# Expert blocks of 32 rows on four column tiles of TensorE, and two early weight loads held for the first gather

## The chip, the cores and the metric

The kernel runs on one core of one Trainium2 chip. The metric is device microseconds of one execution, the median of several runs. TensorE multiplies, VectorE and ScalarE do elementwise work and empty PSUM, GpSimd (POOL in the profile) does the gathers, SyncE (SP) issues most DMAs.

## The reference

Two transformer-like blocks over 512 tokens of width 1024, in float32: FFN, two attentions, FFN, then a convolution and mLSTM mixer, and at the end a mixture of experts. The change lies in the last part. 32 experts, each token goes to two of them:

```python
h = xt @ router weights          # group of 8 experts by argmax, then top 2 in the group
for each expert e, its rows xb:
    a, u = xb @ w_gate[e], xb @ w_up[e]          # 1024 x 512 each
    y = (silu(a) * u) @ w_down[e]                # 512 x 1024
out[token] = x[token] + sum over its 2 experts of gate * y
out = rmsnorm(out)
```

The reference's router sends these inputs to the experts in very uneven parts. In the order in which the kernel takes the experts, they get 6, 21, 0, 109, 2, 150, 1, 61, 6, 82, 3, 61, 6, 90, 3, 55, 4, 6, 1, 46, 2, 22, 8, 34, 7, 8, 0, 129, 5, 59, 2, 35 rows, 1024 in all.

## The kernel before

Everything up to the router is not touched, and is not told here. The experts' rows are cut into blocks of `BS` = 64 rows (`MAX_BLOCKS` at most), a block belongs to one expert. Three sets of buffers (`SETS`, chosen by block number modulo 3) each hold one expert's gate, up and down weights of 2 MB each. The blocks run in laps of three, one for each set. The first three experts open the three sets; the others are laid out down the first set's column, then down the second's, then down the third's, so that all blocks of one expert follow each other in the same set, three apart. A set's weights are loaded again only when the expert of its column changes (`need`); an expert that has several blocks keeps its set for as many laps. With 64 rows there are 37 blocks in 13 laps (39 places, two of them empty).

One block `c` on each engine:

- TensorE: `gate_up(c)` (L1737: 8 contraction chunks, each one matmul for gate and one for up, on two column tiles of 64), `next_rows` (L1658: the gathered rows of block c+1 turned), `down(c-1)` (L1752: 4 chunks by two output halves, again on two column tiles), `turn_products(c)` (L1760: gate and up products of block c turned, 4 transposes).
- ScalarE: copies the products out of PSUM (L1766), copies the result of block c-1 (L1777) and issues its two stores to `y_rows` (L1780), and applies silu (L1771).
- VectorE: scales the turned rows (L1699), hands the next row numbers to GpSimd (L1663), multiplies silu and up (L1792).
- GpSimd: gathers the rows of block c+4 once block c+1's have been turned (L1651).
- SyncE: `load_first(c)` issues gate and up of block c after `gate_up(c-3)`, `load_down(c-1)` issues down of block c-1 after `down(c-4)`. All weight loads stand in this one queue, in that order: gate c, up c, down c-1.

Ahead of the loop SyncE loads the first experts. `load_expert(2, 1, 1)` and `load_expert(2, 2, 2)` are the last of these. The router's counts and places are worked out on VectorE, then `gather(0)` is issued, and block 0 can begin. After the loop GpSimd gathers each token's two results from `y_rows`, VectorE adds them, and the output is stored.

Of the kernel before, what the change touches and what calls it, by code (L numbers as in the profile page):

```python
# [32 lines left out]
BS = 64  # L33
MAX_BLOCKS = N_EXP + 2 * T // BS
SETS = 3
NO_ROW = 8 * T
SLOT_COLS = MAX_BLOCKS + 4
# [89 lines left out]
def build(nc, x_d, cols_d, rows_d, wdense_d, wff_d, wif_d, wr_d, strips_d, experts_d, out_d):  # L127
# [15 lines left out]
    s_y = sem("block_results_stored")  # L143
# [72 lines left out]
    iota_f, tok_id = sb("iota_f", 128), sm(2 * NT)  # L216
# [130 lines left out]
    y_d = nc.dram_tensor("y_rows", (MAX_BLOCKS * BS, D), F32).ap()  # L347
# [38 lines left out]
    def ffn(first_in, first_out, ready, gain):  # L386
# [523 lines left out]
    assert RING * SLOT - WE >= 1024 + 8 * BS and 5 * WE <= BIG - 8 * T  # L910
# [578 lines left out]
    sp.wait_ge(PE.sem, PE.n)  # L1489
    load_expert(2, 1, 1)  # L1490
    sp.wait_ge(s_hrow, NT * 16)
# [12 lines left out]
    quota, steps3, multiples = sm(32), sm(MAX_BLOCKS // SETS), sm(8)  # L1504
# [3 lines left out]
    DV.step(dv.tensor_scalar(multiples, iota_f[:, 1:9], float(BS), None, ALU.mult))  # L1508
# [64 lines left out]
    DV.run(dv.tensor_scalar(nb.bitcast(I32), nb.bitcast(I32), 6, None, ALU.logical_shift_right))  # L1573
# [26 lines left out]
    over = work[:, 256:256 + C2 * 8].rearrange("p (c n) -> p c n", c=C2)  # L1600
    DV.run(dv.tensor_tensor(over, over_last(rank, C2, 8), multiples.unsqueeze(1).to_broadcast([128, C2, 8]), ALU.is_ge))
# [12 lines left out]
    oh_tok, oh_exp = work[:, 1952:1952 + C2 * SLOT_COLS], hi_raw[:, 2 * D:2 * D + C2 * SLOT_COLS]  # L1614
    assert C2 * SLOT_COLS <= 416 and 2 * D + C2 * SLOT_COLS <= 2 * SLOT

# [27 lines left out]
    y_e, gu = ring[:, 0:512], ring[:, 512:1024]  # L1644
    hg, het = ring[:, 1024:1024 + 4 * BS], ring[:, 1280:1280 + 4 * BS]
# [60 lines left out]
    take_rows(0, slice(3, 4)).then_inc(DV.sem, 2)  # L1706
    DV.n += 3

    ac.wait_ge(s_fill, 16)
    ac.sem_inc(s_y, 16)  # L1710

    per = {"pe": 4, "ac": 3, "dv": 3}
# [4 lines left out]
    DV_X, DV_IDX, DV_MUL = range(1, 4)  # L1717
# [5 lines left out]
    turned_h = banks[4].rearrange("p (c m s) -> p c m s", c=4, m=2)  # L1723
# [3 lines left out]
    def gate_up(i, c, rows_next=True):  # L1727
# [17 lines left out]
    def down(i, c, steps=1):  # L1745
# [91 lines left out]
    ac.wait_ge(s_y, laps["ac"] * (32 * SETS) + (32 * (SETS - 1) + 16))
    ac.activation(y_e, results[SETS - 1][:, :], ACT.Copy).then_inc(AC.sem, 1)
    ac.wait_ge(AC.sem, at_step(AC, AC_SILU, laps["ac"], 2) + 1)
    for half in range(2):  # L1840
        ac.dma_start(y_d[bass.ds(laps["ac"] * (SETS * BS) + (SETS - 1) * BS, BS), half * 512:half * 512 + 512],
                     y_e[half * BS:(half + 1) * BS, :]).then_inc(s_y, 16)
# [30 lines left out]
    po.wait_ge(s_y, laps["po"] * (32 * SETS) + (32 * SETS + 16))  # L1873
# [151 lines left out]
```

## Time and profile before

| | us |
|---|---|
| median of 3 runs (lowest, highest) | 2067.76 (2067.05, 2069.86) |
| the profiled execution's own time | 2066.26 |
| its span | 2065.0 |
| TensorE busy in the span | 1878.1 |
| bytes read from HBM | 383.84 MB |

The span is what the profile covers; the execution's own time is 1.3 us longer. Start times in the trace are counted from the span's start. An engine's busy time tells how long it had an instruction under way, not that it was at its limit.

### The profile page before, as it was taken

To read this page: it belongs to the slowest core of one execution; us is meant where nothing else is said; L and a number is where in the kernel's file an instruction comes from. 1 tells how busy PE (TensorE), PEld (TensorE's weight loads), DVE (VectorE), ACT (ScalarE), POOL (GpSimd) and SP (SyncE) were. 2 spreads that over 40 slices of the span, in tenths; PEclk is the share of its full clock that TensorE was granted. 3 is DMA by queue.
4 is the path that set the end of the run, shared out by engine and by line. 5 is a ranking of instruction groups with operands and counts; after the bars stand their busy time and mean duration, and the time that the engine had idled before them with its cause. 6 is when DMAs were issued, how large, how long until landed. Compare 5 with 4: busy or idle time off the path is not lost.

```text
span 2065.0 us, 24162 instructions
## 1 busy us (share of the span) xinstructions
PE 1878.1 (91%) x8560; PEld 1287.1 (62%) x8560; DVE 830.5 (40%) x1150; ACT 415.0 (20%) x749; POOL 976.4 (47%) x505
## 2 busy tenths in 40 slices
PE   5999999989999899999999798987869989998893
PEld 4888888777776678888888576664733333333330
DVE  5444443310344577444443588786330000010003
ACT  3111100100244432111100244441411111111111
POOL 5888887767544378888887433221210000010001
PEclk9999999999999999999999999997769999999996
DMA  3333383322211132332322122211779999999983
GB/s 127 100 92 101 96 333 115 137 82 92 72 52 52 41 92 92 92 102 92 105 98 98 57 72 61 61 52 31 290 251 413 404 411 367 380 408 406 421 366 137
DMA packets 59585, 353.73 MB, mean 171 GB/s; under 512 B 8426, under 2 KB 8810, under 8 KB 47504
## 3 DMA queue, kind: packets, MB, share of 16 engines
q1 hardware_dynamic: 44640, 315.12, 41.8%
q10 hardware_dynamic: 10048, 26.80, 3.4%
q0 software_dynamic: 4848, 11.17, 1.7%
q8 instruction: 29, 0.48, 0.1%
q14 instruction: 20, 0.16, 0.0%
HBM read 383.84 MB, written 27.00 MB: 199 GB/s over the span
## 4 chain that ended last, share of the span: by engine, by line
PE 75%; DVE 11%; DMA 9%; ACT 3%; issue 1%; POOL 1%; ACTq 0%; DVEq 0%; SPq 0%; POOLq 0%
PE bank L457 30%; PE bank L428 12%; PE bank L1737 11%; DMA big<-w_up_in 7%; PE bank L1752 5%; PE bank L689 4%; PE bank L1263 3%; DVE big L1040 3%; PE bank L476 2%; PE bank L1373 2%; PE bank L607 1%; DVE state L1025 1%; PE bank L1658 1%; PE bank L667 1%; PE bank L1760 1%
## 5 line engine op out<-in xcount | busy, mean ns | idle before, releaser
L274 POOL TENSOR_TENSOR weights_hi_parts<-ring,ones 128x1024 fp32r<-128x1024 f32 (+1 forms) x176 | 356.6, 2026 | 302.6 <-PE bank L457 137.2
L276 POOL TENSOR_TENSOR ring_parts<-ring,weights_hi_parts 128x1024 fp32r<-128x1024 f32 (+1 forms) x176 | 473.9, 2693 | 13.8
L457 PE MATMUL bank<-attention_buffers_parts,weights_hi_parts 128*128 128x512 f32 x832 | 328.4, 395 | 28.5 <-POOL ring_parts L276 17.7
L457 PE MATMUL bank<-state_parts,weights_hi_parts 128*128 128x512 f32 x832 | 325.9, 392 | 0.0
L457 PE MATMUL bank<-attention_buffers_parts,ring_parts 128*128 128x512 f32 x832 | 325.8, 392 | 0.0
L1737 PE MATMUL bank<-big,work 128*64 128x512 f32 x1040 | 289.0, 618 | 20.2 <-DMA big<-w_up_in 19.9
L428 PE MATMUL bank<-big_parts,weights_hi_parts 128*128 128x512 f32 x704 | 216.9, 389 | 1.2 <-POOL ring_parts L276 1.2
L457 PEld LDWEIGHTS bank<-attention_buffers_parts,weights_hi_parts 128*128 128x128 f32 x832 | 157.6, 189 | 65.3 <-POOL ring_parts L276 17.7
L1822 POOL TENSOR_TENSOR small<-small 128x1 f32<-128x1 f32 x36 | 7.0, 194 | 393.6 <-DVE small L1663 393.6
L861 POOL TENSOR_TENSOR ring_parts<-ring,weights_hi_parts 128x1024 fp32r<-128x1024 f32 x32 | 81.0, 2534 | 234.1 <-ACT weights_hi_parts L858 234.1
L457 PEld LDWEIGHTS bank<-attention_buffers_parts,ring_parts 128*128 128x128 f32 x832 | 157.4, 189 | 33.2
L457 PEld LDWEIGHTS bank<-state_parts,weights_hi_parts 128*128 128x128 f32 x832 | 157.6, 189 | 32.7 <-issue 0.8
L1737 PEld LDWEIGHTS bank<-big,work 128*64 128x64 f32 x1040 | 91.0, 142 | 133.2 <-issue 133.2
L428 PEld LDWEIGHTS bank<-big_parts,weights_hi_parts 128*128 128x128 f32 x704 | 132.0, 188 | 29.4 <-POOL ring_parts L276 2.0
L428 PE MATMUL bank<-big_parts,ring_parts 128*128 128x512 f32 x352 | 136.9, 389 | 0.0
L1699 DVE TENSOR_TENSOR work<-bank,cols 128x512 f32<-128x512 f32 x39 | 27.0, 692 | 243.3 <-PE bank L1658 243.3
L403 DVE TENSOR_TENSOR work<-bank,token_scale 128x512 f32<-128x512 f32 x44 | 30.4, 691 | 199.4 <-PE bank L457 199.4
L1040 DVE SCALAR_TENSOR_TENSOR big<-big,cols 128x512 f32<-128x512 f32 x120 | 106.4, 927 | 6.4 <-ACT big L1034 5.3
L1792 DVE TENSOR_TENSOR ring<-ring,bank 128x256 f32<-128x256 f32 x39 | 16.4, 421 | 222.0 <-ACT ring L1771 222.0
L1737 PE MATMUL bank<-attention_buffers,work 128*64 128x512 f32 x208 | 95.2, 612 | 8.9 <-DMA big<-w_up_in 8.1
L312 DVE TENSOR_TENSOR big_parts<-work,big_parts 128x512 f32 (+1 forms) x44 | 82.9, 1883 | 42.3 <-ACT big_parts L310 42.3
L1752 PE MATMUL bank<-state,ring 128*64 128x512 f32 x416 | 96.6, 607 | 2.6 <-DVE ring L1792 2.6
(363 smaller groups left out, 2681.7 us busy)
## 6 DMA issues: line engine op xcount, KB each, us to landing
ring<-wdense_in SPq DMA_DIRECT2D x176, 512.0 KB, 3.5
big<-w_up_in SPq DMA_DIRECT2D x39, 2048.0 KB
state<-w_down_in SPq DMA_DIRECT2D x27, 2048.0 KB
big<-w_gate_in SPq DMA_DIRECT2D x26, 2048.0 KB
attention_buffers<-w_gate_in SPq DMA_DIRECT2D x13, 2048.0 KB
ring<-w_down_in SPq DMA_DIRECT2D x13, 2048.0 KB
ring<-wff_in SPq DMA_DIRECT2D x32, 704.0 KB, 4.0
y_rows<-big ACTq DMA_DIRECT2D x1, 12288.0 KB, 41.4
```

The costliest lines, as they stand in the source:

```text
L274: po.tensor_tensor(hi, raw, ones[:, 0:1].to_broadcast([128, words]), ALU.mult).then_inc(PO.sem, 1)
L276: po.tensor_tensor(lo, raw, hi.bitcast(F32), ALU.subtract) \
L312: return DV.step(dv.tensor_tensor(lo, raw, hi.bitcast(F32), ALU.subtract))
L428: m = pe.matmul(bank, x, y_, start=t + k + n == 0, stop=t == 1 and k == h - 1 and n == 2)
L457: m = pe.matmul(out, x, y_, start=j + n == 0, stop=j == len(pairs) - 1 and n == len(ts) - 1)
L476: m = pe.matmul(banks[t][:, :], x, y_, start=k + n == 0, stop=k == KD - 1 and n == len(ts) - 1)
L689: m = pe.matmul(banks[7][:, :], x, y_, start=k + t == 0, stop=k == KD - 1 and t == 2, skip_group_check=True)
L861: lo_made[n] = PO.step(po.tensor_tensor(lo, raw, hi.bitcast(F32), ALU.subtract))
L1040: last = DV.step(dv.scalar_tensor_tensor(dst, src, w, dst, ALU.mult, ALU.add))
L1263: m = pe.matmul(banks[bank][:, :], x, y_, start=k + j == 0, stop=k == KD - 1 and j == 2, skip_group_check=True)
L1737: m = pe.matmul(first_products[b][m_ * BS:(m_ + 1) * BS, :], xet[:, k * BS:(k + 1) * BS], sets[b][m_][:, k * D_EXP:(k + 1) * D_EXP], start ...
L1752: m = pe.matmul(results[b][half * BS:(half + 1) * BS, :], het[:, k * BS:(k + 1) * BS], sets[b][2][:, k * D + half * 512:k * D + half * 512 ...
```

## The change

Blocks have 32 rows instead of 64. By the counts above there are then 52 blocks in 18 laps (54 places). Each block's gate and up products run on four column tiles of 32: gate and up of an even chunk and gate and up of the odd chunk beside it; the down product likewise, two output halves for an even and an odd chunk. So a block still has 16 and 8 matmuls, but the sums of even and odd chunks stand in different partitions of PSUM and must be added: for gate and up by a matmul with `fold` (two stacked identities) in place of the transposes; for the result by a copy of the odd half on ScalarE (`act_odd`) and an addition on VectorE (`dve_result`). The stores of a block wait for that addition. Each set has its own result buffer and store semaphore. The first two down loads of sets 1 and 2 wait for the first gather; before, the first of them waited for TensorE alone and the second for the normalised rows' stores.

```diff
@@ -30,10 +30,12 @@
 N_EXP, N_GRP, PER_GRP, D_EXP = 32, 4, 8, 512
 
 
-BS = 64
-MAX_BLOCKS = N_EXP + 2 * T // BS
+BS = 32
+MAX_BLOCKS = N_EXP + 2 * T // BS - 1
+BLOCK_SHIFT = 5
 SETS = 3
 NO_ROW = 8 * T
+Y_ROWS = -(-MAX_BLOCKS * BS // 128) * 128
 SLOT_COLS = MAX_BLOCKS + 4
 RING = 4
 SMALL = 2048
...
@@ -213,7 +215,8 @@
     for q in (PE, AC, DV):
         q.wait(c_ready)
         q.eng.wait_ge(s_cols, 16)
-    iota_f, tok_id = sb("iota_f", 128), sm(2 * NT)
+    iota_f, tok_id, fold = sb("iota_f", 128), sm(2 * NT), sm(2 * BS)
+    PO.run(po.tensor_tensor(fold, ident[:, 0:2 * BS], ident[:, 2 * BS:4 * BS], ALU.add))
...
@@ -1487,8 +1490,8 @@
         po.dma_start(h_d[t * 128:(t + 1) * 128, :], h_tok[:, t * D:(t + 1) * D]).then_inc(s_hrow, 16)
 
     sp.wait_ge(PE.sem, PE.n)
+    sp.wait_ge(s_gath[0], 16)
     load_expert(2, 1, 1)
-    sp.wait_ge(s_hrow, NT * 16)
     load_expert(2, 2, 2)
 
 
...
@@ -1641,8 +1646,9 @@
 
     xe = (work[0:BS, 0:D], work[0:BS, 1536:1536 + D], hi_raw[0:BS, D:2 * D])
     xet = work[:, D:D + KD * BS]
-    y_e, gu = ring[:, 0:512], ring[:, 512:1024]
-    hg, het = ring[:, 1024:1024 + 4 * BS], ring[:, 1280:1280 + 4 * BS]
+    y_e = [ring[0:2 * BS, b * 512:(b + 1) * 512] for b in range(SETS)]
+    y_odd = work[0:2 * BS, 2560:3072]
+    gu, hg, het = hi_raw[:, 2048:2560], hi_raw[:, 2560:2560 + 4 * BS], hi_raw[:, 2688:2688 + 4 * BS]
     idx = [sm(1) for _ in range(SETS)]
     laps = {}
     lo, hi = 2 * T // BS // SETS - 1, MAX_BLOCKS // SETS - 1
...
@@ -1730,12 +1737,15 @@
         pe.wait_ge(DV.sem, at_step(DV, DV_X, i, c - 1))
         for m_ in range(2):
             pe.wait_ge(s_wexp[m_][b], i * 16 + (16 * (c // SETS) + 16))
-        for k in range(KD):
-            if k == KD - 1 and rows_next:
+        for k in range(0, KD, 2):
+            if k == KD - 2 and rows_next:
                 pe.wait_ge(s_gath[(c + 1) % SETS], i * 16 + (16 * ((c + 1) // SETS) + 16))
-            for m_ in range(2):
-                m = pe.matmul(first_products[b][m_ * BS:(m_ + 1) * BS, :], xet[:, k * BS:(k + 1) * BS],
-                              sets[b][m_][:, k * D_EXP:(k + 1) * D_EXP], start=k == 0, stop=k == KD - 1)
+            for odd in range(2):
+                for m_ in range(2):
+                    p = (2 * odd + m_) * BS
+                    m = pe.matmul(first_products[b][p:p + BS, :], xet[:, (k + odd) * BS:(k + odd + 1) * BS],
+                                  sets[b][m_][:, (k + odd) * D_EXP:(k + odd + 1) * D_EXP], start=k == 0, stop=k == KD - 2,
+                                  tile_position=(0, p))
         m.then_inc(PE.sem, 1)
 
     def next_rows(c):
...
@@ -1747,17 +1757,19 @@
         b = c % SETS
         pe.wait_ge(DV.sem, at_step(DV, DV_MUL, i, c))
         pe.wait_ge(s_wexp[2][b], i * 16 + (16 * (c // SETS) + (32 if b == 2 else 16)))
-        for k in range(4):
-            for half in range(2):
-                m = pe.matmul(results[b][half * BS:(half + 1) * BS, :], het[:, k * BS:(k + 1) * BS],
-                              sets[b][2][:, k * D + half * 512:k * D + half * 512 + 512], start=k == 0, stop=k == 3)
+        for k in range(0, 4, 2):
+            for odd in range(2):
+                for half in range(2):
+                    p, o = (2 * odd + half) * BS, (k + odd) * D + half * 512
+                    m = pe.matmul(results[b][p:p + BS, :], het[:, (k + odd) * BS:(k + odd + 1) * BS], sets[b][2][:, o:o + 512],
+                                  start=k == 0, stop=k == 2, tile_position=(0, p))
         m.then_inc(PE.sem, steps)
 
     def turn_products(i, c, steps=1):
 
         pe.wait_ge(AC.sem, at_step(AC, AC_GU, i, c))
         for k in range(4):
-            m = pe.transpose(banks[4][:, k * 128:(k + 1) * 128], gu[:, k * 128:(k + 1) * 128], ident[:, :])
+            m = pe.matmul(banks[4][:, k * 2 * BS:(k + 1) * 2 * BS], gu[:, k * 128:(k + 1) * 128], fold, start=True, stop=True)
         m.then_inc(PE.sem, steps)
 
     def act_copy(i, c):
...
@@ -1770,15 +1782,27 @@
         ac.wait_ge(PE.sem, at_step(PE, PE_HT, i, c))
         ac.activation(hg3, turned_h[:, :, 0, :], ACT.Silu).then_inc(AC.sem, steps)
 
-    def act_result(i, c):
+    def act_odd(i, c):
 
         ac.wait_ge(PE.sem, at_step(PE, PE_D, i, c + 1))
-        ac.wait_ge(s_y, i * (32 * SETS) + (32 * c + 16))
-        ac.activation(y_e, results[c % SETS][:, :], ACT.Copy).then_inc(AC.sem, 1)
-        ac.wait_ge(AC.sem, at_step(AC, AC_Y, i, c + 1))
+        ac.activation(y_odd, results[c % SETS][2 * BS:4 * BS, :], ACT.Copy).then_inc(AC.sem, 1)
+
+    def act_store(i, c):
+
+        ac.wait_ge(DV.sem, at_step(DV, DV_Y, i, c + 1))
+        store(i, c)
+
+    def store(i, c):
+
         for half in range(2):
             ac.dma_start(y_d[bass.ds(i * (SETS * BS) + c * BS, BS), half * 512:half * 512 + 512],
-                         y_e[half * BS:(half + 1) * BS, :]).then_inc(s_y, 16)
+                         y_e[c % SETS][half * BS:(half + 1) * BS, :]).then_inc(s_y[c % SETS], 16)
+
+    def dve_result(i, c, steps=1):
+
+        dv.wait_ge(AC.sem, at_step(AC, AC_Y, i, c + 1))
+        dv.wait_ge(s_y[c % SETS], i * 32 + (32 * (c // SETS) + 16))
+        dv.tensor_tensor(y_e[c % SETS], results[c % SETS][0:2 * BS, :], y_odd, ALU.add).then_inc(DV.sem, steps)
 
     def dve_rows(i, c):
 
```

TensorE, one block in the loop, of before. `big` and `attention_buffers` hold gate and up weights, `ring` and `state` down weights, `work` the turned rows:

```order
L1737 MATMUL bank<-big,work 64x512 x13
L1737 MATMUL bank<-big,work 64x512 [waits block_rows_gathered_2]
L1737 MATMUL bank<-big,work 64x512
L1658 MATMUL bank<-ident,weights_hi 128x64 x8
L1748 REGISTER_ALU
L1752 MATMUL bank<-ring 64x512 [waits expert_weights_down_0,dve_steps]
L1752 MATMUL bank<-ring 64x512 x7
L1758 REGISTER_ALU
L1760 MATMUL bank<-ident,ring 128x128 [waits act_steps]
L1760 MATMUL bank<-ident,ring 128x128 x3
L1730 REGISTER_ALU
```

And of the changed kernel, the same place:

```order
L1746 MATMUL bank<-big,work 32x512 x11
L1746 MATMUL bank<-big,work 32x512 [waits block_rows_gathered_2]
L1746 MATMUL bank<-big,work 32x512 x3
L1664 MATMUL bank<-ident,weights_hi 128x32 x8
L1758 REGISTER_ALU
L1764 MATMUL bank<-ring,weights_hi 32x512 [waits expert_weights_down_0,dve_steps]
L1764 MATMUL bank<-ring,weights_hi 32x512 x7
L1770 ISA
L1772 MATMUL bank<-small,weights_hi 128x64 [waits act_steps]
L1772 MATMUL bank<-small,weights_hi 128x64 x3
L1737 REGISTER_ALU
```

The numbers of matmuls are the same, with 32 columns in place of 64 in the array; the wait for the next gather stands four matmuls ahead of the end instead of two; the four transposes by `ident` are four matmuls with `fold` (in `small`).

ScalarE, one block in the loop, of before (copy of the products, copy of the result, two stores, silu):

```order
L1766 ACTIVATE ring<-bank 128x512 [waits pe_steps]
L1775 REGISTER_ALU
L1776 ISA [waits pe_steps]
L1777 ACTIVATE ring<-bank 128x512 [waits block_results_stored]
L1778 ISA
L1780 ISA [waits act_steps]
L1780 DMA y_rows<-ring 64x512
L1780 ISA
L1780 DMA y_rows<-ring 64x512
L1770 REGISTER_ALU
L1771 ACTIVATE ring<-bank 128x256 [waits pe_steps]
```

And of the changed kernel (copy of the products, copy of the odd half, silu, two stores):

```order
L1778 ACTIVATE weights_hi<-bank 128x512 [waits pe_steps]
L1787 REGISTER_ALU
L1788 ACTIVATE work<-bank 64x512 [waits pe_steps]
L1782 REGISTER_ALU
L1783 ACTIVATE weights_hi<-bank 128x128 [waits pe_steps]
L1792 REGISTER_ALU
L1798 ISA [waits dve_steps]
L1798 DMA y_rows<-ring 32x512
L1798 ISA
L1798 DMA y_rows<-ring 32x512
```

Silu has moved ahead of the stores, and the stores wait for VectorE.

SyncE, ahead of the loop, of before (the last loads; `state<-w_down_in` are the down weights of sets 1 and 2):

```order
L918 DMA big<-w_up_in 128x4096 [waits pe_steps]
L918 DMA ring<-w_down_in 128x4096
L918 DMA big<-w_up_in 128x4096
L1435 DMA weights_hi<-rows_in 128x1024
L918 DMA state<-w_down_in 128x4096 [waits pe_steps]
L918 DMA state<-w_down_in 128x4096 [waits normalised_rows_stored]
```

And of the changed kernel:

```order
L921 DMA big<-w_up_in 128x4096 [waits pe_steps]
L921 DMA ring<-w_down_in 128x4096
L921 DMA big<-w_up_in 128x4096
L1438 DMA weights_hi<-rows_in 128x1024
L921 DMA state<-w_down_in 128x4096 [waits block_rows_gathered_0,pe_steps]
L921 DMA state<-w_down_in 128x4096
```

The first of the two now waits for the first gathered block, and the second follows it without a wait of its own.

## Rows read from the trace of the kernel before

**Rows 1.** The page's slices of the span, 51.6 us each: TensorE and DMA share.
```profile
PE   5999999989999899999999798987869989998893
...
DMA  3333383322211132332322122211779999999983
```

**Rows 2.** Windows by stage; columns: length, busy time per engine, PEclk, DMA share, GB/s.
```profile
1520.00:1534.00 14.00, 9.53 (x40) 3.48 (x40) 0.74 (x2) 0.00 (x0) 1.12 (x2) 0.69 0.29 64
1534.00:1646.00 112.00, 108.06 (x554) 39.78 (x553) 11.64 (x30) 15.20 (x29) 11.28 (x20) 0.99 1.00 398
...
1700.00:1870.00 170.00, 170.00 (x866) 61.28 (x863) 17.04 (x44) 22.43 (x43) 16.93 (x30) 1.00 0.99 384
1870.00:2006.00 136.00, 118.20 (x563) 44.30 (x564) 10.90 (x28) 15.19 (x29) 7.90 (x14) 0.94 1.01 419
2006.00:2033.00 27.00, 23.71 (x108) 8.03 (x104) 1.58 (x4) 3.75 (x7) 0.00 (x0) 0.94 0.11 28
```

**Rows 3.** DMA queues from 1534 to 2010 us: packets, MB, share of 16 engines.
```profile
q1 hardware_dynamic: 12096, 176.17, 91.0%
q10 hardware_dynamic: 5760, 9.44, 5.3%
```

**Rows 4.** The chain that ended last, three of its stretches of DMA.
```profile
1638.30 40.73 DMA big<-w_up_in
1679.17 8.68 PE bank L1737 x32
...
1854.15 34.34 DMA big<-w_up_in
...
1966.80 32.79 DMA big<-w_up_in
```

**Rows 5.** The same chain, one block: gate and up, next rows, down, next block.
```profile
1559.59 7.02 PE bank L1737 x32
1566.61 0.64 PE bank L1658 x8
1567.24 3.58 PE bank L1752 x16
1571.41 7.02 PE bank L1737 x32
```

**Rows 6.** Timeline of TensorE inside one block's gate and up.
```profile
1753.06 0.59 PE L1737 MATMUL bank<-attention_buffers,work 128*64 128x512 f32 x1
1753.07 0.59 PE L1737 MATMUL bank<-big,work 128*64 128x512 f32 x1
1753.49 0.59 PE L1737 MATMUL bank<-attention_buffers,work 128*64 128x512 f32 x1
```

**Rows 7.** Timeline of the weight loads: 128 columns, fp32, at half and at full clock.
```profile
1511.64 3.49 PEld L457 LDWEIGHTS bank<-weights_hi,ones 128*128 128x128 f32 x16
...
1660.06 0.42 PEld L1760 LDWEIGHTS bank<-ident,ring 128*128 128x128 f32 x4 [0.81 <-issue]
```

**Rows 8.** A window of 10 us without a store in it.
```profile
1680.00:1690.00 10.00, 10.00 (x48) 3.69 (x46) 0.74 (x2) 0.60 (x1) 0.20 (x1) 0.88 1.02 431
```

**Rows 9.** Timeline around the first gather, and the last gathers' median to landing (us).
```profile
1495.00 17.89 SPq L918 DMA_DIRECT2D state<-w_down_in  x2
...
1513.48 1.03 POOL L1651 DMA_INDIRECT work<-h_rows,small  x1 [15.05 <-DMA h_rows<-state]
...
1523.62 1.11 PE L1658 MATMUL bank<-ident,work 64*128 64x64 f32 x8 [8.31 <-DMA work<-h_rows,small]
...
1534.56 0.34 SPq L920 DMA_DIRECT2D attention_buffers<-w_gate_in  x1
...
big<-y_rows,small POOLq DMA_INDIRECT x8, 5.9
```

**Rows 10.** Timeline of the last output halves on TensorE and their copy on ScalarE.
```profile
2026.94 5.35 PE L1752 MATMUL bank<-state,ring 128*64 128x512 f32 x16 [2.58 <-DVE ring L1792]
...
2032.41 0.60 ACT L1838 ACTIVATE ring<-bank 128x512 f32<-128x512 f32 x1 [6.12 <-PE bank L1752]
```

More of the change, by code:

```diff
@@ L142, in build @@
     s_wexp = [[sem(f"expert_weights_{n}_{b}") for b in range(SETS)] for n in ("gate", "up", "down")]
-    s_y = sem("block_results_stored")
+    s_y = [sem(f"block_results_stored_{b}") for b in range(SETS)]
     s_fill = sem("block_results_cleared")
@@ L909, in build @@
     WE = KD * D_EXP
-    assert RING * SLOT - WE >= 1024 + 8 * BS and 5 * WE <= BIG - 8 * T
+    assert RING * SLOT - WE >= SETS * 512 and 5 * WE <= BIG - 8 * T
     sets = ((att[:, 0:WE], big[:, 4 * WE:5 * WE], ring[:, RING * SLOT - WE:RING * SLOT]),
@@ L1503, in build @@
     m8, i8 = sm(NT * 8), sm(NT * 8)
-    quota, steps3, multiples = sm(32), sm(MAX_BLOCKS // SETS), sm(8)
+    quota, steps3, multiples = sm(32), sm(MAX_BLOCKS // SETS), sm(T // BS - 1)
     DV.wait(numbered)
@@ L1572, in build @@
     DV.run(dv.tensor_scalar(nb.bitcast(I32), nb, float(BS - 1), None, ALU.add))
-    DV.run(dv.tensor_scalar(nb.bitcast(I32), nb.bitcast(I32), 6, None, ALU.logical_shift_right))
+    DV.run(dv.tensor_scalar(nb.bitcast(I32), nb.bitcast(I32), BLOCK_SHIFT, None, ALU.logical_shift_right))
     DV.run(dv.tensor_copy(nb, nb.bitcast(I32)))
@@ L1599, in build @@
     DV.run(dv.tensor_reduce(rank, chosen.rearrange("p (c e) -> p c e", e=32), axis=AX.X, op=ALU.add))
-    over = work[:, 256:256 + C2 * 8].rearrange("p (c n) -> p c n", c=C2)
-    DV.run(dv.tensor_tensor(over, over_last(rank, C2, 8), multiples.unsqueeze(1).to_broadcast([128, C2, 8]), ALU.is_ge))
+    n_over = T // BS - 1
+    over = work[:, 256:256 + C2 * n_over].rearrange("p (c n) -> p c n", c=C2)
+    DV.run(dv.tensor_tensor(over, over_last(rank, C2, n_over), multiples.unsqueeze(1).to_broadcast([128, C2, n_over]),
+                            ALU.is_ge))
     DV.run(dv.tensor_reduce(rdiv, over, axis=AX.X, op=ALU.add))
@@ L1613, in build @@
     oh_row, oh_slot = work[:, 512:512 + C2 * BS], work[:, 1536:1536 + C2 * SLOT_COLS]
-    oh_tok, oh_exp = work[:, 1952:1952 + C2 * SLOT_COLS], hi_raw[:, 2 * D:2 * D + C2 * SLOT_COLS]
-    assert C2 * SLOT_COLS <= 416 and 2 * D + C2 * SLOT_COLS <= 2 * SLOT
+    oh_tok, oh_exp = work[:, 2072:2072 + C2 * SLOT_COLS], hi_raw[:, 2 * D:2 * D + C2 * SLOT_COLS]
+    assert 512 + C2 * BS <= 1536 and C2 * SLOT_COLS <= 536 and 2 * D + C2 * SLOT_COLS <= 2 * SLOT
     def by_slot(x):
@@ L1705, in build @@
     keep_rows().then_inc(DV.sem, 1)
-    take_rows(0, slice(3, 4)).then_inc(DV.sem, 2)
-    DV.n += 3
+    take_rows(0, slice(3, 4)).then_inc(DV.sem, 3)
+    DV.n += 4
     ac.wait_ge(s_fill, 16)
-    ac.sem_inc(s_y, 16)
-    per = {"pe": 4, "ac": 3, "dv": 3}
+    for b in range(SETS):
+        ac.sem_inc(s_y[b], 16)
+    per = {"pe": 4, "ac": 3, "dv": 4}
     base = {"pe": PE.n, "ac": AC.n, "dv": DV.n}
@@ L1829, in build @@
             act_copy(i, c)
-            act_result(i, c - 1)
+            act_odd(i, c - 1)
             act_silu(i, c)
+            act_store(i, c - 1)
     for c in range(1, SETS):
         act_copy(laps["ac"], c)
-        act_result(laps["ac"], c - 1)
+        act_odd(laps["ac"], c - 1)
         act_silu(laps["ac"], c)
+        act_store(laps["ac"], c - 1)
     ac.wait_ge(PE.sem, at_step(PE, PE_HT, laps["ac"], 2) + 1)
[L1837 to L1842, printed above, removed]
+    ac.activation(y_odd, results[2][2 * BS:4 * BS, :], ACT.Copy).then_inc(AC.sem, 1)
+    ac.wait_ge(DV.sem, at_step(DV, DV_MUL, laps["ac"], 2) + 1)
+    store(laps["ac"], 2)
     dve_rows(0, 0)
-    dve_mul(0, 0)
+    dve_mul(0, 0, 2)
     with dv.Fori(0, laps["dv"]) as i:
@@ L1848, in build @@
             dve_rows(i, c)
+            dve_result(i, c - 1)
             dve_mul(i, c)
     dve_rows(laps["dv"], 1)
+    dve_result(laps["dv"], 0)
     dve_mul(laps["dv"], 1)
-    dve_mul(laps["dv"], 2, 3)
+    dve_result(laps["dv"], 1, 3)
+    dve_mul(laps["dv"], 2)
+    dv.wait_ge(AC.sem, at_step(AC, AC_SILU, laps["dv"], 2) + 1)
+    dv.wait_ge(s_y[2], laps["dv"] * 32 + 16)
+    dv.tensor_tensor(y_e[2], results[2][0:2 * BS, :], y_odd, ALU.add).then_inc(DV.sem, 1)
     gate_up(0, 0)
@@ L1870, in build @@
     down(laps["pe"], 2)
-    po.wait_ge(s_y, laps["po"] * (32 * SETS) + (32 * SETS + 16))
+    for b in range(SETS):
+        po.wait_ge(s_y[b], laps["po"] * 32 + 48)
     po.wait_ge(PO.sem, laps["po"] * SETS + gathers_begun)
```

12 lines of the change are left out of this document (6 added, 6 removed).

## The prediction

> **What bounds the kernel now.** I read the page's slices first [rows 1]. TensorE shows 9 nearly everywhere, and DMA is low until the expert loop, the last fifth, where it shows 9 as well. So I went on with windows by stage [rows 2]: from 1534 to 2006 us the DMA share is 0.99 to 1.01 in every stage, whether TensorE is busy throughout (1700 to 1870) or not (118 of 136 us from 1870 on). The queues say what is moved [rows 3]: queue 1, SyncE's weight loads, moves 176.17 MB. That is 84 loads of 2.097 MB, or 28 sets filled anew with three loads each. Last, the chain of waits [rows 4]: it passes three times into a load of up weights that was issued 33 to 41 us before TensorE could use it. A 2 MB load takes about 5 us, so these loads stood behind some seven others. The loop is bound by a stream of loads that never runs dry, and TensorE, though busy, runs ahead or beside it. After the stream ends near 2006 [rows 2] TensorE works alone until the last down product ends at 2026.94 + 5.35 = 2032.3 [rows 10].
>
> **The stream's price.** From the first issue, 1534.6 [rows 9], to 2006 it takes 471 us. A window without a store moves 431 GB/s [rows 8], so a load costs 4.87 us and 84 of them 409. The other 62 us are the price of 39 blocks' stores and gathers, 1.6 us a block (5.3% of the stretch is the store queue's own packets [rows 3]).
>
> **A block on TensorE, before.** Gate and up 7.02, next rows 0.64, down 3.58, and the turned products the rest: from 1559.59 to 1571.41 one block takes 11.82 us [rows 5], so the last part is 0.58. Inside gate and up the two column tiles start together and a pair of instructions follows every 0.43 us, two to a matmul [rows 6]: a pair of matmuls costs 0.86, eight pairs 6.88.
>
> **A block after.** If four tiles run together as the two do, gate and up are four groups of 0.86, 3.44, and with the same 0.15 of edges 3.59; down 1.72 + 0.14 = 1.86; next rows stays at 0.64, since eight weight loads set it. The `fold` matmuls are no transposes; each needs two passes, so eight loads of 128 columns. Such a load takes 3.49/16 = 0.22 us at half clock, and a transpose's 0.42/4 = 0.105 at full clock [rows 7]. That bounds the step by 0.84 and 1.75; I take 1.2, nearer to the lower because the 0.22 was at half clock. The block is 3.59 + 0.64 + 1.86 + 1.2 = 7.3 us. ScalarE's and VectorE's added work (a copy and an addition of 64 x 512) lies beside the next block's 3.59 us of gate and up, and the stores are behind silu; I cost them nothing inside the loop. If that cover were gone it would be about 1.3 us a block, two PSUM passes like ScalarE's 0.60 [rows 10].
>
> **What does not change.** The bytes. By the row counts, blocks of 32 are 52 in 18 laps, but a set is still filled anew 28 times, 84 loads. By laps (from the second on) the numbers of sets filled anew are 3,2,3,2,2,1,2,3,3,3,2,2 before and 3,2,0,2,3,2,0,1,1,0,3,3,1,3,2,1,1 after. The first expert of set 0 with 109 rows now has 4 blocks, the one with 150 has 5, the one with 129 in set 2 has 5. While they hold their sets nothing can be loaded there. Before, such laps took TensorE 35 us each and the backlog bridged them. Now a lap takes 22 us, but its loads are missing altogether.
>
> **The stores.** Their bytes fall from 39 x 256 KB to 54 x 128 KB; gathered rows are the same 1024. The charge of a block on the stream is between 0.8 (all by bytes and rows) and 1.6 (all by number of transfers); I take 1.0.
>
> **The front.** The two held loads free the DMA engines for the normalised rows and the first gather. The gather is issued at 1513.48 and its rows are used at 1523.62 [rows 9], 10.1 us; the last gathers, beside no load, land in 5.9 [rows 9]. VectorE's index work is about even (a 512-wide step becomes 256, three 416-wide ones 536). So block 0's gate and up starts near 1513.2 + 5.9 + 2 = 1521 and ends near 1526; before, its end released the load at 1534.56 [rows 9]. The held loads then run from about 1519.5 to 1530, and the stream goes on from there at once, 5 us earlier than before.
>
> **The sum**, as a chain of stretches. It uses that SyncE issues up of block c ahead of down of block c-1, so the loads up to up(c) leave out two downs.
> 1. Stream-bound from 1530 to block 8: 13 loads x 4.87, 5 block charges, 1.5 to land: 1599.8.
> 2. The sets of lap 4 can be filled only after block 10's gate and up: 2 x 7.3, plus 3.6, plus 1.4 for a half-clock start (a gate and up after a stall took 8.68 in place of 7.02 [rows 4]), plus 2 to issue: 1621.4. The stream has then been dry for about 9 us.
> 3. Stream-bound to block 20: 19 loads, 10 charges, 1.5: 1725.4.
> 4. TensorE-bound through the long experts to block 30's gate and up: 10 x 7.3 + 2.6 + 3.6 + 2: 1806.6. Only two sets are filled in it, so the stream is dry for about 40 us in two parts.
> 5. Stream-bound to block 47: 34 loads, 17 charges, 1.5: 1990.7.
> 6. TensorE-bound to the end: 7 x 7.3 + 2.6, the last down 1.9, and 2.0 because it waits for VectorE's product with nothing beside it (2.58 before [rows 10]): 2048.3.
>
> That is 16.0 later than 2032.3. Behind it the added result costs 0.8 (VectorE's addition after ScalarE's copy). The gathers and the end stay. 2066.26 + 16.8 = 2083.1 for the profiled execution, which lies 1.5 under the median, so 2084.6: **2085 us**. The gains (5 at the front, 18 of charges, 9 of a shorter end) are smaller than the 49 us in which the stream stands dry.
>
> **The rivals.**
> - *The four tiles do not run four abreast.* Rows 6 show only two. If a group takes 1.14 instead of 0.86 (three at a time), the block is 9.0, and the 19 blocks of stretches 2, 4 and 6 add 32: 2117. The Trainium skill bears on it: "TensorE: Matmul & The Clock Gate", Part 3, gives 3.07 times for four row tiles and 2.38 for three column tiles. By an estimate from that page a group takes 1.12, the block 8.9, and the time would be 2115; no trace here shows four tiles. If fp32 tiles go only two at a time, the block is 12.4, TensorE bounds all 54: 1522.8 + 54 x 12.4 + 5.6 = 2198, and the time 2234.
> - *The charge is by transfers*: 1.6 a block, 32 blocks x 0.6: 2104.
> - *The block is at its floor*: `fold` at 0.66 like the transposes and no edges, 6.44. 19 x 0.86 less: 2069, no change by measurement.
> - *Faster: stores and gathers of small blocks ride nearly free on the stream.* Of the 1.6 us, 0.6 are a store's own bytes; the rest may be the two engines' queues in each other's way, which may vanish with 64 KB less in each transfer. It acts in stretches 1, 3 and 5. At 0.2 a block the time is 2085 - 32 x 0.8 = 2059; it decides from 0.33 downward. Against it: the same number of rows is gathered and 38% more transfers are made.
>
> **How the numbers follow.** Likeliest 0.54 (2085, its own range 2073 to 2099 from `fold`, 7 less to 10 more, and a charge of 0.8 to 1.1); three abreast 0.17; two abreast 0.04; by transfers 0.07; floor 0.07; free ride 0.11. A difference under 0.2%, 4 us, is about what a measurement of this kernel can't tell from none. The faster case is the free ride; no change is the floor and an edge of the likeliest; the rest is slower. The range goes from 2064, which takes in the floor, to 2116, which takes in most of three abreast. Out of it are the free ride, two abreast and half of three abreast: about 0.2.
>
> **What the profile after would show.** TensorE: groups of four every 0.43 us and a block of 7.3 where it isn't waiting; `fold` near 1.2. Stream: 84 loads again, first at about 1530, and DMA near zero around 1612 to 1621, 1735 to 1750 and 1790 to 1807. TensorE waits for up weights some 110 us in all (527 us of loop, less 54 x 7.3 and the half-clock starts). If the dry stretches are there but shorter, the block is shorter than I said; if they are missing, my reading of how long a set is held is wrong, and with it the forecast.

## The result, and the profile after

| | us, median (lowest, highest) |
|---|---|
| before, 4 runs | 2067.97 (2067.05, 2069.86) |
| changed, 4 runs | 2089.07 (2087.22, 2091.78) |
| changed, the profiled execution | 2091.78, span 2090.5 |

The ratio of changed to before is 1.0102, 95% interval 1.0084 to 1.0119: slower by 21 us. The forecast was 2085, its own range 2073 to 2099. All six stretches of its chain can be found in the trace. The three that the stream of loads bounds are longer than forecast, the three that TensorE bounds are about as long or shorter. Below, the stream is called dry while no load is under way, because every set still holds an expert in use.

The windows of the changed kernel by stage (length, busy time of each engine, PEclk, DMA share, GB/s):

```profile
1530.00:1605.00 75.00, 56.03 (x436) 21.88 (x428) 9.37 (x27) 10.14 (x21) 7.73 (x14) 0.84 1.01 408
1605.00:1635.00 30.00, 28.53 (x260) 11.98 (x264) 5.62 (x17) 5.82 (x13) 4.42 (x8) 1.00 0.66 256
1635.00:1735.00 100.00, 65.58 (x512) 25.31 (x504) 11.77 (x34) 11.95 (x25) 8.82 (x16) 0.82 1.01 410
1735.00:1820.00 85.00, 83.02 (x741) 33.39 (x741) 15.60 (x44) 16.33 (x34) 12.12 (x22) 0.97 0.60 219
1820.00:2005.00 185.00, 127.46 (x999) 49.84 (x1001) 22.53 (x64) 23.34 (x48) 17.65 (x32) 0.82 1.01 415
2005.00:2058.00 53.00, 52.24 (x452) 20.37 (x444) 9.39 (x26) 10.29 (x21) 3.32 (x6) 0.96 0.66 256
```

Read the DMA share against TensorE's busy time. In the first, third and fifth row the DMA engines are full and TensorE is idle a quarter to a third of the time. In the second and fourth it is the other way round: TensorE is busy nearly throughout, and the DMA engines stand still for 30 x 0.34 + 85 x 0.40 = 44 us. Before, it was 0.99 or more in every stage from 1534 to 2006 [rows 2]; only windows of 10 us show it lower, 0.84 to 0.97 in five of them between 1744 and 1814. Windows of 10 us in the two stages of the changed kernel show where its stream is dry:

```profile
1610.00:1620.00 10.00, 9.28 (x83) 3.75 (x84) 1.82 (x6) 1.69 (x4) 2.12 (x4) 1.00 0.43 170
1620.00:1630.00 10.00, 10.00 (x95) 4.26 (x98) 2.32 (x6) 2.12 (x5) 1.17 (x3) 1.00 0.51 163
1740.00:1750.00 10.00, 10.00 (x96) 4.02 (x92) 1.70 (x5) 2.06 (x4) 1.09 (x2) 1.00 0.11 31
1750.00:1760.00 10.00, 10.00 (x92) 4.27 (x88) 2.23 (x7) 2.34 (x5) 2.21 (x4) 1.00 0.33 91
...
1800.00:1810.00 10.00, 10.00 (x96) 4.32 (x92) 2.32 (x6) 2.34 (x5) 2.02 (x3) 1.00 0.06 14
```

The chain that ended last, one block in the fourth stage (start, duration, what), answers to [rows 5]:

```profile
1745.52 3.57 PE bank L1746 x32
1749.10 0.61 PE bank L1664 x8
1749.71 1.85 PE bank L1764 x16
1751.56 1.03 PE bank L1772 x8
1752.60 3.57 PE bank L1746 x32
```

Gate and up 3.57, the next rows 0.61, down 1.85, `fold` 1.03: a block is 7.07 to 7.08 us, against 11.82 before. The timeline of TensorE inside one gate and up answers to [rows 6]:

```profile
1809.06 0.62 PE L1746 MATMUL bank<-attention_buffers,work 128*32 128x512 f32 x1
1809.07 0.62 PE L1746 MATMUL bank<-big,work 128*32 128x512 f32 x1
1809.07 0.62 PE L1746 MATMUL bank<-attention_buffers,work 128*32 128x512 f32 x1
1809.08 0.62 PE L1746 MATMUL bank<-big,work 128*32 128x512 f32 x1
1809.51 0.59 PE L1746 MATMUL bank<-attention_buffers,work 128*32 128x512 f32 x1
```

Four instructions, one on each column tile, start within 0.02 us, and the next four come 0.45 us later (then every 0.43). Before, two started together and the next pair came after 0.42 to 0.43.

TensorE's waits for up weights (us in total, times, longest):

```profile
PE bank L1746 <- DMA big<-w_up_in: 109.7, 21, 8.3
```

The chain where it last leaves the stream:

```profile
1973.87 29.79 DMA big<-w_up_in
2003.79 6.46 PE bank L1746 x32
```

The timeline of SyncE, the issue that ends the long dry stretch:

```profile
1813.02 0.34 SPq L923 DMA_DIRECT2D attention_buffers<-w_gate_in  x1
```

TensorE waited 109.7 us in 21 waits for up weights (28.0 us in 10 before). The last is over at 2003.79, and the chain then stays on TensorE until the last down product ends at 2058.1.

The queues from 1525 to 2030 us (packets, MB, share of 16 engines), which answer to [rows 3]:

```profile
q1 hardware_dynamic: 11954, 174.10, 84.7%
q10 hardware_dynamic: 4608, 6.30, 3.7%
q0 software_dynamic: 2408, 4.09, 2.6%
```

### The profile page after: what moved, and what is told of

It is laid out like the page before. It is cut to its first block, busy times and chain, and to the rows that moved or that the text cites. A ratio compares the mean times of both kernels' runs of the same rounds, so it can differ in the third digit from the quotient of the medians.

```text
span 2090.5 us, 27387 instructions
## 1 busy us (share of the span) xinstructions
PE 1827.7 (87%) x9676; PEld 1282.0 (61%) x9676; DVE 862.6 (41%) x1249; ACT 432.7 (21%) x794; POOL 991.6 (47%) x536
## 4 chain that ended last, share of the span: by engine, by line
PE 68%; DMA 15%; DVE 11%; ACT 3%; issue 1%; POOL 1%; SPq 0%; DVEq 0%; ACTq 0%; POOLq 0%
PE bank L460 30%; DMA big<-w_up_in 13%; PE bank L431 11%; PE bank L1746 7%; PE bank L692 4%; PE bank L1266 3%; DVE big L1043 3%; PE bank L1764 2%; PE bank L479 2%; PE bank L1376 2%; DMA state<-w_down_in 1%; PE bank L1772 1%; PE bank L610 1%; DVE state L1028 1%; PE bank L670 1%
## 5 line engine op out<-in xcount | busy, mean ns | idle before, releaser
L1746 PE MATMUL bank<-big,work 128*32 128x512 f32 x1440 | 235.7, 696 | 78.4 <-DMA big<-w_up_in 78.4
L1705 DVE TENSOR_TENSOR work<-bank,cols 128x256 f32<-128x256 f32 x54 | 22.9, 425 | 341.8 <-PE bank L1664 341.8
L1746 PEld LDWEIGHTS bank<-big,work 128*32 128x32 f32 x1440 | 59.0, 125 | 165.9 <-issue 162.4
L1746 PE MATMUL bank<-attention_buffers,work 128*32 128x512 f32 x288 | 77.4, 686 | 31.9 <-DMA big<-w_up_in 31.3
L1778 ACT ACTIVATE weights_hi<-bank 128x512 f32<-128x512 f32 x54 | 32.3, 598 | 346.5 <-PE bank L1746 346.5
L313 ACT ACTIVATE big_parts<-work 128x512 f32 (+1 forms) x44 | 27.9, 633 | 287.4 <-DVE work L408 287.4
```

Of the source, the lines that this page charges most:

```text
L1746: m = pe.matmul(first_products[b][p:p + BS, :], xet[:, (k + odd) * BS:(k + odd + 1) * BS], sets[b][m_][:, (k + odd) * D_EXP:(k + odd + 1) ...
```

## The experiments

Each ratio is that to the kernel before, which ran beside the experiment. Where an experiment is set against the changed kernel, the two medians stem from separate sets of runs; the medians of the kernel before in these sets lie between 2066.9 and 2068.4, so a difference of 1 or 2 us between sets means nothing.

**1. The held loads alone, on the kernel before.**

```diff
     sp.wait_ge(PE.sem, PE.n)
+    sp.wait_ge(s_gath[0], 16)
     load_expert(2, 1, 1)
-    sp.wait_ge(s_hrow, NT * 16)
     load_expert(2, 2, 2)
```

> The kernel before with the two held loads alone. If the chain of the prediction is right, block 0 starts about 5 us earlier, the first load of the loop too, and the stream of loads, which bounds this kernel nearly to its end, ends 4 to 5 us earlier: 2063 (2061 to 2065). If holding two loads back only moves 10 us of transfers from before the gather to behind it, the stream is to finish at the same time: 2068, no change.

Measured: 2064.98 (2062.07 to 2066.24), ratio 0.9981 (0.9972 to 0.9990), so 3.9 us faster by the ratio and 3.4 by the medians. The timeline on SyncE and TensorE (start, duration, instruction, idle time before it and its releaser):

```profile
1519.71 1.11 PE L1658 MATMUL bank<-ident,work 64*128 64x64 f32 x8 [2.02 <-DMA work<-h_rows,small]
...
1519.74 1.16 SPq L918 DMA_DIRECT2D state<-w_down_in  x2
...
1532.06 0.35 SPq L920 DMA_DIRECT2D attention_buffers<-w_gate_in  x1
```

The wait for the first gathered rows falls from 8.31 [rows 9] to 2.02 us, and the first load of the loop is issued at 1532.06 instead of 1534.56, in an execution that was 2.4 us later than the other even ahead of the router. (VectorE's division on line 1211 starts at 1440.23 before and at 1442.59 here, as the next two rows show.)

```profile
1440.23 3.35 DVE L1211 RECIPROCAL state<-state 128x512 f32<-128x512 f32 x1 [0.77 <-ACT state L1208]
```

```profile
1442.59 3.35 DVE L1211 RECIPROCAL state<-state 128x512 f32<-128x512 f32 x1 [0.77 <-ACT state L1208]
```

Counted from the division, the loop's stream begins 4.9 us earlier. So the chain of the prediction holds for the front, and the rival (10 us only moved) falls.

**2. The changed kernel with the two loads where they were.** The diff is that of experiment 1, the other way round.

> The changed kernel with the two loads issued where they were before. If the held loads give the stream its 5 us in the changed kernel too, it comes out about 5 us slower, 2094 (2091 to 2096); the dry stretches that TensorE sets move along with block 0, so nothing of it is lost. If the holding is worth nothing: 2089.

Measured: 2092.31 (2087.62 to 2092.77), ratio 1.0108 (1.0092 to 1.0123), 3.2 us above the changed kernel's 2089.07 by the medians, but only some 1 us by the ratios, whose intervals overlap. The sign agrees with experiment 1; what the held loads are worth in the changed kernel isn't settled by the times. The trace does show the front later: the first load of the loop is issued at 1532.60 instead of 1526.72. TensorE's wait for the first rows is back:

```profile
1524.29 1.06 PE L1664 MATMUL bank<-ident,work 32*128 32x32 f32 x8 [6.13 <-DMA work<-h_rows,small]
```

**3 and 4. The experts in a spread order, in the changed kernel and in the kernel before.** The order in which experts are taken is a table on the host, which the router's columns and the experts' weights share. Within each of the four groups it can be any permutation. In the old order the experts with 109 and 150 rows stand at places 3 and 5 (counted from 0). By the row counts they follow each other in set 0, in laps 1 to 4 and 6 to 10 (from 0), while the other two sets hold long experts as well; in laps 3, 7 and 10 all three sets keep their expert, and nothing is loaded. In this one the experts with 129, 109, 150 and 90 rows stand at 7, 11, 13 and 17, and every lap has a refill:

```diff
-    by_turns = np.arange(N_EXP).reshape(N_GRP, PER_GRP).T.reshape(-1)
+    by_turns = np.array([0, 8, 16, 26, 5, 12, 22, 30, 3, 14, 19, 24, 4, 9, 18, 25] +
+                        [6, 11, 20, 27, 2, 13, 23, 29, 7, 15, 17, 28, 1, 10, 21, 31])
```

> The changed kernel with the experts taken in another order, so that the long ones lie apart: the same 52 blocks in 18 laps, the same first three experts, the same 28 refills with 84 loads, the same stores, but refills by lap of 3,1,1,2,2,1,2,1,1,3,2,1,2,2,1,1,2, with no lap without one. My theory (the stream of loads ran dry for some 49 us): the dry stretches vanish, and the time falls by 38 to 46 us to 2047 (2041 to 2053), below the kernel before. Rival 1, the small transfers' charge: nothing changes in their number, 2089. Rival 2, TensorE's work of 54 small blocks, half-clock starts among them: nothing changes in it, 2085 to 2089.

> The control: the kernel before with that same order. Its stream was never dry for more than some microseconds, since its laps are 35 us of TensorE work each and refills are more even by lap; so the order should be worth little: 2066 (2058 to 2070). If the order helps for a reason of its own that has nothing to do with blocks of 32 (other rows together, another end), it gains as much here as the changed kernel does: 2025.

Measured: the changed kernel takes 2037.02 (2034.57 to 2038.56), ratio 0.9844 (0.9829 to 0.9859); the kernel before 2058.71 (2056.61 to 2060.80), ratio 0.9949 (0.9934 to 0.9964). The order is worth 52 us to the changed kernel and some 10 us to the other. Windows of the changed kernel in this order:

```profile
1530.00:1635.00 105.00, 87.73 (x748) 35.71 (x748) 16.75 (x48) 17.61 (x36) 13.24 (x24) 0.92 1.01 404
1635.00:1735.00 100.00, 83.75 (x732) 33.99 (x728) 15.70 (x45) 16.15 (x33) 12.14 (x22) 0.93 0.99 397
1735.00:1820.00 85.00, 65.02 (x552) 26.67 (x544) 12.72 (x36) 13.21 (x27) 9.91 (x18) 0.90 1.01 416
1820.00:1945.00 125.00, 109.05 (x915) 43.35 (x919) 19.73 (x56) 20.55 (x42) 15.45 (x28) 0.92 1.00 402
```

The dry stretches are gone: the DMA share is 0.99 or more up to 1945. Blocks, loads and stores are as many as in the changed kernel, so neither a charge of small transfers nor TensorE's work could have given 52 us. Both gains are larger than I expected (38 to 46, and 2). With nothing else changed the two kernels now stand the other way round: 2037.0 against 2058.7, and blocks of 32 are 21.7 us faster. This order is fitted to the row counts of this input. It is an experiment on the cause and not a setting for other inputs.

**5 and 6. Both kernels without the loads of the loop.** In the table of refills a threshold that no expert's number reaches:

```diff
-    tables = DV.run(dv.scalar_tensor_tensor(need[:, SETS:SLOT_COLS].bitcast(I32), exp1[:, SETS:SLOT_COLS], 0.0, changed,
+    tables = DV.run(dv.scalar_tensor_tensor(need[:, SETS:SLOT_COLS].bitcast(I32), exp1[:, SETS:SLOT_COLS], 99.0, changed,
```

> The changed kernel without the 84 loads of the loop (the table of refills is all zero, so every block runs on the first three experts' weights; the blocks, gathers and stores are all there). It shows TensorE's own time for 54 blocks of 32. By my theory a block is 7.07 us whatever stands around it, so the loop ends at 1520.8 + 5.7 + 53 x 7.07 + 5.5, near 1906 in place of 2058: about 1938 (1933 to 1945). The rival that small blocks cost TensorE more than their stage in the trace shows would end nearer to 1960.

> The kernel before without its 84 loads in the loop (all blocks on the first three experts' weights). 39 blocks of 11.82 us: the loop ends near 1991 to 1997 in place of 2032, so 2027 to 2033. The difference from the changed kernel without loads, about 90 us, is what four tiles and blocks of 32 are worth on TensorE alone; if it is that large, TensorE's work isn't where the changed kernel lost.

Measured, one execution each: 1938.47 for the changed kernel, 2027.74 for the kernel before. A window of each, first the changed kernel's:

```profile
1640.00:1740.00 100.00, 100.00 (x907) 41.18 (x903) 19.73 (x56) 21.17 (x43) 16.21 (x29) 1.00 0.12 32
```

```profile
1640.00:1740.00 100.00, 100.00 (x514) 36.40 (x514) 10.05 (x26) 13.83 (x26) 10.14 (x18) 1.00 0.14 34
```

TensorE is busy all the time, and the chain repeats 3.57, 0.61, 1.85, 1.03 in the one and 7.02, 0.64, 3.58, 0.59 in the other. Without the loads the changed kernel is 89 us faster. TensorE's work is therefore not where the time was lost; ScalarE's copy, VectorE's addition and the stores lie wholly beside it. With its loads the kernel before is only 40 us above its TensorE time, and the changed one 151 us.

**7 and 9. Both kernels without the stores of the loop.**

```diff
-        for half in range(2):
-            ac.dma_start(y_d[bass.ds(i * (SETS * BS) + c * BS, BS), half * 512:half * 512 + 512],
-                         y_e[c % SETS][half * BS:(half + 1) * BS, :]).then_inc(s_y[c % SETS], 16)
+        ac.sem_inc(s_y[c % SETS], 32)
```

> The changed kernel without its 108 stores of results in the loop (their semaphore is counted up in their place; y_rows stays cleared). If a block's stores charge the stream 0.9 us (what a charge of 1.4 a block with gathers fits), 24 us go: 2065 (2060 to 2069). At my predicted charge of 1.0 with gathers (0.6 for the stores) it would be 16 us: 2073. If the stores ride free and the loads themselves are slower than 4.87 us: 2087 to 2089.

> The kernel before without its 78 stores of the loop. Two stores of 128 KB a block against two of 64 KB in the changed kernel: if the charge goes by transfers, 0.9 a block, 21 us go, less some 3 for a stream that then runs dry sooner: 2047 to 2050. If it goes by bytes, a block's stores charge twice what they do in the changed kernel, and 30 us or more would be free, up to where TensorE bounds: 2040 or less.

Measured: 2079.06 (2078.03 to 2079.71) for the changed kernel, 10 us less; 2042.36 (2037.46 to 2044.12), ratio 0.9872 (0.9852 to 0.9891) for the kernel before, 24.5 to 26.5 us less. The edit shown is the changed kernel's; in the kernel before all 78 stores are left out in the same way. Experiment 9 lies between my two expectations, nearer to that by bytes. My estimate of 24 for the changed kernel was wrong, and the charge by transfers with it: there are more transfers in the changed kernel, and they cost less than half. What fits is the queue's own share. Before, queue 10 holds 5.3% of 476 us [rows 3], 25.2 us, and that is what its absence gives back. In the changed kernel it holds 3.7% of 505 us, 18.7 us; 32 of 54 blocks lie in stretches where the DMA engines are full, which leaves 11 of them, and 10 come back. That fits stores that cost nothing while the stream is dry. Nor do the stores make the loads dearer: from 1525 to 2000 us of experiment 7 queue 1 moves 168.42 MB (80.3 loads) at a share of 87.3%, which is 5.16 us a load without any store, and experiment 9 gives 5.19 (174.66 MB, 95.8% of the 451 us from 1534).

**8. The changed kernel with half as wide stores.**

```diff
-            ac.dma_start(y_d[bass.ds(i * (SETS * BS) + c * BS, BS), half * 512:half * 512 + 512],
-                         y_e[c % SETS][half * BS:(half + 1) * BS, :]).then_inc(s_y[c % SETS], 16)
+            ac.dma_start(y_d[bass.ds(i * (SETS * BS) + c * BS, BS), half * 512:half * 512 + 256],
+                         y_e[c % SETS][half * BS:(half + 1) * BS, 0:256]).then_inc(s_y[c % SETS], 16)
```

> The changed kernel with each store half as wide: 256 of the 512 columns, so 32 KB in place of 64 KB in as many transfers (the other columns of y_rows stay cleared). Leaving the stores out gave 10 us in the changed kernel and 24.5 in the kernel before. If a store is paid by its bytes, half of the 10 us goes: 2084 (2082 to 2086). If it is paid as a transfer, nothing goes: 2089. If short rows cost more than their bytes, it is 2089 or above.

Measured: 2086.22 (2084.21 to 2086.78), ratio 1.0091 (1.0075 to 1.0108). It is 2.9 us below the changed kernel, but the intervals of the two ratios overlap widely. The queue's row is clearer than the time:

```profile
q10 hardware_dynamic: 4704, 3.22, 2.1%
```

Half the bytes in as many packets take 2.1% in place of 3.7%, so mostly the bytes are paid, and some of the transfer too. In the time it can't be told apart from nothing with certainty.

**10 and 11. The experts in a bunched order, in both kernels.** Here the experts with 90, 129, 150 and 109 rows stand close together, at places 5, 7, 9 and 11:

```diff
+    by_turns = np.array([0, 8, 16, 29, 3, 11, 23, 30, 2, 9, 20, 24, 5, 15, 21, 31] +
+                        [1, 12, 17, 27, 6, 14, 18, 25, 7, 10, 22, 28, 4, 13, 19, 26])
```

> The changed kernel with the experts in a third order, in which three of the four long ones follow each other: refills by lap 3,2,3,2,0,1,3,2,0,2,1,1,3,3,2,1,0; again the same blocks, loads and first three experts. If the held sets are the cause, it works in this direction too: by the same chain (load 5.15, charge 0.6, block 7.07) the loop ends 36 us later than in the changed kernel, 2125 (2113 to 2135). If the gain of the spread order came from something else, such as which rows lie together, there is no reason for a loss: 2089.

> The control: the kernel before in this bunched order. Its refills by lap are 3,3,2,2,3,2,2,2,3,3,2,1, nearly even, so it should lose far less than the changed kernel: 2077 (2068 to 2082). A loss as large as the changed kernel's, 36 us, would say that blocks of 32 have nothing to do with it.

Measured: 2125.57 (2123.18 to 2126.51), ratio 1.0279 (1.0262 to 1.0296) for the changed kernel; 2078.30 (2076.32 to 2079.02), ratio 1.0050 (1.0033 to 1.0067) for the kernel before. Both came out within 1.5 us of the number expected. But the changed kernel does not make the same loads in this order, as the expectation has it. Its own list of refills by lap adds up to 29, not 28: by the row counts the expert with 150 rows lies across the seam of two sets, with one block in set 1 and four at the end of set 0, and is loaded twice. The rows of queue 1 over the whole span, from the two pages of the profile, show it; the changed kernel's first:

```profile
q1 hardware_dynamic: 44640, 315.12, 41.4%
```

```profile
q1 hardware_dynamic: 45072, 321.41, 41.2%
```

The difference is 6.29 MB, three loads of 2.097 MB. At 5.15 us each they are some 15 of the 36 us; the other 21 are left for the order. The kernel before makes 84 loads in either order and loses 11. Two windows of the changed kernel show the stream dry for 24 and 22 us:

```profile
1635.00:1735.00 100.00, 80.26 (x652) 31.11 (x648) 14.05 (x40) 14.68 (x30) 11.03 (x20) 0.86 0.76 304
...
1820.00:1950.00 130.00, 109.10 (x920) 44.28 (x912) 20.77 (x60) 21.42 (x44) 16.53 (x30) 0.90 0.83 335
```

So the clean comparison is that of experiment 3: the same 52 blocks and 84 loads take the changed kernel 2037 or 2089 us, by nothing but the order in which the sets come free. Experiment 10 points the same way, with three loads more.

**12. A spread order with one refill less.** If none of the first three experts is without rows, three refills fall to the first loads instead of two:

```diff
+    by_turns = np.array([4, 15, 23, 31, 7, 9, 18, 26, 0, 12, 17, 25, 6, 10, 16, 27] +
+                        [2, 8, 20, 30, 1, 13, 19, 28, 3, 14, 21, 24, 5, 11, 22, 29])
```

> The changed kernel in a spread order in which none of the first three experts is without rows, so that one refill fewer is needed: 27, 81 loads, by lap 2,1,2,2,2,1,1,1,2,3,1,1,1,2,2,1,2. My theory: one refill of 15 us less in a stream that bounds nearly everything, so 10 to 16 us below the other spread order's 2037: 2024 (2018 to 2030). If TensorE bounds the spread order by now, one refill less gives little: 2033 to 2037.

Measured: 2022.84 (2022.40 to 2023.10), ratio 0.9783 (0.9767 to 0.9800). That is 14.2 us under the first spread order, for three loads of 5.15. The stream still bounds this version. It is the fastest of the orders, 44 us under the kernel before in the old order (which was not run in this one), and again fitted to this input.

## Why the prediction came out as it did

The mechanism was right, and the runs show it: blocks of 32 are cheap on TensorE, but a long expert holds its set through laps in which nothing can be loaded, and TensorE, now faster than the stream, has no backlog to bridge them. The stream was forecast to stand dry for 49 us and does for 44. The sizes were off in both directions, and the small error of the median is partly luck: for the profiled execution the forecast was 2083.1 and it took 2091.8, 8.7 more, but it was the longest of the four. The chain's stretches in it:

| stretch | forecast, us | measured, us |
|---|---|---|
| 1, from 1530 to block 8 | 69.8 | 75.6 (2.9 of it a late execution) |
| 2, until sets come free | 21.6 | 21.0 |
| 3, to block 20 | 104.0 | 110.3 |
| 4, through the long experts | 81.2 | 78.0 |
| 5, to block 47 | 184.1 | 188.8 |
| 6, to the end of the last down | 57.6 | 54.3 |

The ends of stretches 1, 3 and 5 are the starts of gate and up on TensorE at 1605.62, 1736.98 and 2003.79. Stretches 2 and 4 end 2 us after the issues at 1624.64 and 1813.02. The rows of the first two:

```profile
1605.62 2.78 PE L1746 MATMUL bank<-big,work 128*32 128x512 f32 x24 [0.80 <-DMA big<-w_up_in]
...
1736.98 1.93 PE L1746 MATMUL bank<-big,work 128*32 128x512 f32 x8 [5.59 <-DMA big<-w_up_in]
```

- **What bounds before: right.** Experiment 6 puts TensorE 40 us under the kernel's time, experiment 9 takes the stores' 25 us out of the stream, and they come back in full. That the stream "never runs dry" was a little too strong: shares of 0.84, 0.91, 0.96, 0.97 and 0.97 in windows of 10 us from 1744 to 1814 add up to some 4 us.
- **The stream's price: the load was sized too low, the charge too high.** I took 4.87 us from one window at 431 GB/s. The queue's own row gives 91.0% of 476 us for 84 loads [rows 3], 5.16; after, 84.7% of 505 us for 83 loads, 5.15. Of the 62 us that I spread over the blocks as 1.6 a block, 24 were the loads' own (84 x 0.29), and experiments 7 and 9 show that they stay without the stores. In the changed kernel a block's stores and gathers take (3.7% + 2.6%) of 505 us over some 52 blocks, 0.6, not 1.0.
- **The count: wrong by two.** Listing the loads in the order in which SyncE issues them gives 20 for stretch 3 and 35 for stretch 5, not 19 and 34. With these counts and prices stretch 3 is 20 x 5.15 + 10 x 0.6 + 1.5 = 110.5 (measured 110.3), and stretch 5 is 192.0 (188.8). Together that is 14.4 over the forecast, where 11.0 were measured: 9.7 for the two loads left out, 15.4 for dearer loads (55 of them), less 10.8 for a cheaper charge (27 blocks). That the forecast was only 4 us low owes something to errors that offset each other, and so does the wait for up weights, forecast at some 110 us and measured at 109.7: the loop took 537 us instead of 527, and 54 blocks 382 instead of 394, so 22 us more than I had reckoned went into slow starts and other waits, which I had sized too small.
- **Four abreast: right.** The rows at 1809 show it, so the rivals with three and two abreast fall. The Trainium skill, "TensorE: Matmul & The Clock Gate", Part 3, gives 3.07 times for four row tiles and 2.38 for three column tiles. It has no figure for four column tiles, and my estimate from its factors does not agree with the trace: the 1.12 us for two passes are 0.86, since a group of four takes the 0.43 us that a group of two took. No run shows one tile alone, so the factor against a single tile isn't measured here.
- **`fold`: 1.03 to 1.04 for 1.2,** which with down and the next rows makes a block 7.07 instead of 7.3. It accounts for most of stretches 2, 4 and 6: 19 blocks x 0.23 = 4.4 of the 7.1 us by which they are shorter. The rest wasn't taken apart.
- **What goes in parallel: right.** VectorE's addition and ScalarE's copy cost nothing in the loop (experiment 5). Behind the loop I had charged 0.8 us; the execution's own time is 33.7 us after the last down, before it was 34.0.
- **The front: right in time, by two errors that offset each other.** Gate and up of block 0 starts at 1520.75 (forecast near 1521), although the gather was issued at 1516.16, 2.9 us after the forecast's, for it landed in 2.9 us instead of 5.9. The 2.9 late are there from before the router on: the division at 1440.23 before starts at 1443.10 in this execution, and lies between 1440.2 and 1443.2 in all other profiled executions, of either kernel. Of the 5 us for the stream's start 3 to 4 reach the end in the kernel before (experiment 1); for the changed kernel experiment 2 leaves it open.
- **The faster rival: the wrong mechanism, half a truth.** Stores of small blocks are cheaper than I priced them (0.3 a block by experiment 7), but the "free" part was already in the loads' own price, so it didn't decide.

Not settled: why experiment 3 gained 52 us and not 46. The chain with the corrected prices (5.15 and 0.6), worked out after that run, gives 53. Experiment 10's number, set down from the same chain before it ran, was met within 1 us, which speaks for those prices. Also open is how much of experiment 10's loss an order with 84 loads would have shown.

## What to carry to other kernels

Where a stream of loads into a few buffers bounds a kernel, faster compute is worth nothing while the stream is full, and it takes away the backlog that bridges the laps in which no buffer comes free. So write down the refills by lap before and after: with 84 loads in both orders, the zeros and ones among them decided here between 2037 and 2089 us. Add the list up as well: an item on the seam of two buffers is loaded twice, as in experiment 10. Price a transfer by its queue's share of the whole stretch over its count, not by the best window, and list the loads one by one in issue order before counting them.

## What the runs showed of the hardware

- Four column tiles of 32 in fp32 run fully abreast: four 512-wide passes take the 0.43 us that two took on two tiles of 64.
- A 2 MB load holds the DMA engines for 5.15 to 5.19 us on average over the loop, with stores beside it or without (experiments 7 and 9).
- The stores cost their queue's share of the full stream: without 78 stores of 128 KB the time falls by 24.5 to 26.5 us, the share said 25.2. Without 108 stores of 64 KB it falls by 10.
- After a wait for weights TensorE runs slower: the gate and up at 2003.79, after 5.40 us of waiting, takes 6.46 us, where 3.57 is the rule, and the granted clock from 2003.8 to 2009.0 is 0.50, the lower level of 1.2 GHz. In the stages in which it waits the clock is 0.82 to 0.84 on average. By the chain the 2.9 us count at the start of a stretch that TensorE bounds; that they cost nothing while the stream is the bound is not shown by a run of its own.
